# Gate projections by seven block products, and the inner rows' transposes moved into the experts' products

## The reference

```python
proj = u @ w_in                                   # u: 640 x 1024
qkv, z, b_raw, a_raw, hy, gates = jnp.split(proj, _split_points(IN_SPLITS), -1)
...
gate_a, gate_b = jnp.split(jax.nn.sigmoid(gates), 2, -1)          # 2 x 1024 channels
mixed = (gate_a * (o_a @ w_up_a) + gate_b * (o_b @ w_up_b)) @ w_out
...
hid = jax.nn.silu(jnp.einsum('becd,edf->becf', xs, w_gate)) * jnp.einsum('becd,edf->becf', xs, w_up)
ys = jnp.einsum('becf,efd->becd', hid, w_down) * aff[..., None].astype(u.dtype)
```

## Time and profile before

| | |
|---|---|
| Times of the kernel before | 1490.21 us median of 3 runs (1488.09 to 1490.8) |
| Profiled execution | 1486.47 us, span 1484.7 us |
| TensorE busy | 1385.1 us (93% of the span) |
| VectorE busy | 562.7 us (38%) |
| ScalarE busy | 247.1 us (17%) |
| HBM traffic | 201 GB/s over the span |
| Mean granted TensorE clock | 0.978 |

### The profile page before, as it was taken

How to read it: one execution, slowest core, us unless ns; L and a number is a source line. 1 busy time by engine, 2 the same in 40 slices (tenths; PEclk the granted TensorE clock), 3 DMA queues, 4 the chain that set the end, 5 groups by cost and what they waited for, 6 DMA issues and landing times.

```text
span 1484.7 us, 24301 instructions
## 1 busy us (share of the span) xinstructions
PE 1385.1 (93%) x10696; PEld 746.9 (50%) x10696; DVE 562.7 (38%) x1258; ACT 247.1 (17%) x479; POOL 71.3 (5%) x63
## 2 busy tenths in 40 slices
PE   6999999998999999999999984999999999999991
PEld 2455554657888875556555442443433433433430
DVE  5223237546666641103003675222233322222236
ACT  4311122234223332100000022000010000000010
POOL 0000000000000000000000001111111111111110
PEclk9999999999999999999999996999999999999996
DMA  9732212410000001232022046899999999999984
GB/s 383 336 114 105 90 60 86 170 49 24 2 2 2 2 16 48 123 126 115 26 87 76 39 176 266 296 398 388 393 397 400 400 398 395 398 397 392 401 323 152
DMA packets 32027, 298.92 MB, mean 201 GB/s; under 512 B 3435, under 2 KB 7659, under 8 KB 15580
## 3 DMA queue, kind: packets, MB, share of 16 engines
q1 hardware_dynamic: 20876, 270.93, 45.3%
q0 software_dynamic: 7680, 17.11, 4.6%
q10 hardware_dynamic: 3408, 9.96, 1.7%
HBM read 280.69 MB, written 17.30 MB: 201 GB/s over the span
## 4 chain that ended last, share of the span: by engine, by line
PE 64%; DVE 4%; ACT 1%; DMA 1%; issue 1%; DVEq 0%; POOLq 0%
PE bank L531 63%; ACT front L1205 1%; PE bank L926 1%; DVE hbuf L1731 1%; DVE front L1585 0%; DVE hbuf L1881 0%; DVE stats L1879 0%; DMA y_dram<-front,misc 0%; DMA front<-u_dram,misc 0%; DVE misc L1782 0%; PE bank L472 0%; DMA hbuf<-y_dram 0%; DVE misc L1780 0%; DVE front L1783 0%; DVE front L1576 0%
## 5 line engine op out<-in xcount | busy, mean ns | idle before, releaser
L531 PE MATMUL bank<-front,ring 128*128 128x512 f32 (+1 forms) x1736 | 490.6, 443 | 1.8 <-DVE front L1295 0.9
L531 PE MATMUL bank<-ring,front 128*32 128x256 f32 (+3 forms) x3312 | 427.4, 458 | 2.2 <-DVE front L1837 2.2
L531 PEld LDWEIGHTS bank<-front,ring 128*128 128x128 f32 (+1 forms) x1736 | 265.7, 190 | 230.2 <-issue 224.3
L531 PEld LDWEIGHTS bank<-ring,front 128*32 128x32 f32 (+3 forms) x3312 | 178.9, 124 | 248.6 <-issue 208.5
L531 PE MATMUL bank<-front 128*32 128x256 f32 (+3 forms) x2976 | 271.9, 352 | 9.1 <-ACT front L1205 4.7
L531 PEld LDWEIGHTS bank<-front 128*32 128x32 f32 (+3 forms) x2976 | 163.2, 138 | 112.3 <-issue 86.7
L1861 DVE TENSOR_TENSOR front<-bank,front 128x512 f32<-128x512 f32 x16 | 11.1, 691 | 275.3 <-PE bank L531 275.3
L1846 DVE STREAM_TRANSPOSE front<-front 32x256 f32<-32x256 f32 x192 | 83.4, 434 | 5.5
L1374 DVE SCALAR_TENSOR_TENSOR front<-bank,pk,front 128x511 f32<-128x511 f32 x64 | 32.2, 545 | 99.4 <-ACT front L1009 98.8
L1585 DVE COPY_PREDICATED front<-ck,bank 128x256 f32<-128x256 uint32 (+1 forms) x120 | 52.7, 443 | 24.1 <-PE bank L531 21.7
L1201 ACT ACTIVATE front<-bank 128x512 f32<-128x512 f32 x16 | 9.6, 597 | 274.8 <-PE bank L531 274.8
(11 more groups left out here) (274 smaller groups left out, 886.7 us busy)
## 6 DMA issues: line engine op xcount, KB each, us to landing
ring<-w_e_gate_dram SPq DMA_DIRECT2D x32, 2048.0 KB, 15.2
ring<-w_e_up_dram SPq DMA_DIRECT2D x32, 2048.0 KB, 14.7
front<-w_e_down_dram SPq DMA_DIRECT2D x32, 2048.0 KB, 15.4
ring<-w_in_dram SPq DMA_DIRECT2D x11, 2048.0 KB, 7.9
ring<-w_mod_dram SPq DMA_DIRECT2D x10, 2048.0 KB, 12.9
front<-w_mod_dram SPq DMA_DIRECT2D x2, 2048.0 KB, 29.2
ring<-w_out_dram SPq DMA_DIRECT2D x2, 2048.0 KB, 7.6
h_spill<-hbuf ACTq DMA_DIRECT2D x1, 2560.0 KB, 13.8
```

Of the source, the lines that this page charges most:

```text
L531: return pe.matmul(out, lhsT, rhs, start=(k == 0), stop=(k == n - 1))
```

## The change

For the gates, the product of `uT` and a weight half-chunk (256 channels, a "unit") is split into two by two blocks: tokens in two halves of 320, input channels in two halves of 512, output channels in two blocks of 128. Instead of eight block products there are seven (`factors`), each 4 k-steps of 320 columns, taken from sums of blocks: S1 to S4 of the activations, made once, and T1 to T4 of the weights, made for every unit by `weight_sums`. VectorE also adds the seven results into the four blocks of `sig` (`gate_sums`), reading banks 0 to 3 in turn, and ScalarE takes the sigmoids in place. S1 and S2 lie where `h` is loaded back to, so that load is issued after the last product. In the experts, the `hd` transposes go ahead of the sixth k-step of the up `prompt` product, the `hdc` transposes ahead of the third k-step of the down `sample` product; two semaphores become one.

```diff
@@ -278,6 +279,44 @@
         mixedT = reg(W0 + 5120, 5120).rearrange("p (b t) -> p b t", b=KB)
...
+        HT, HK = TOK // 2, KB // 2
+        Z_DONE, GATE_UNITS = 28, 8
+        A11, A12, A21, A22 = (uT[:, HK * j:HK * j + HK, HT * i:HT * i + HT] for i in range(2) for j in range(2))
+        S1, S2 = (hbuf[:, 2560 + HK * HT * i:2560 + HK * HT * (i + 1)].rearrange("p (k t) -> p k t", k=HK) for i in range(2))
+        S3 = A21
+        S4 = misc[:, TOK:TOK + HK * HT].rearrange("p (k t) -> p k t", k=HK)
+        t_areas = [reg(W0 + 7680 + 512 * i, 512) for i in range(5)] + [prompt_f_all[:, 0:512]]
+        t_areas = [a.rearrange("p (k n) -> p k n", k=HK) for a in t_areas]
+        GATES = ("ga0", "gb0", "ga1", "gb1")
+
+        def quadrants(g):
+            w, u = wslot(CH[GATES[g // 2]][0]), g % 2
+            return [[w[:, HK * i:HK * i + HK, P * (2 * u + j):P * (2 * u + j) + P] for j in range(2)] for i in range(2)]
+
+        def column_sums(g):
+            T1, T2, T4 = t_areas[3 * (g % 2):3 * (g % 2) + 3]
+            return T1, T2, quadrants(g)[0][1], T4
+
+        def factors(g):
+            (B11, _, ), (B21, B22) = quadrants(g)
+            T1, T2, T3, T4 = column_sums(g)
+            return (A11, B11), (S2, T2), (S1, T1), (S3, T3), (S4, B22), (A22, T4), (A12, B21)
+
+        def sums_ready(g):
+            return 6 if g == 0 else 12 * g
+
+        def unit_begin(g):
+            return 12 + 12 * g - (4 if g == GATE_UNITS - 1 else 0)
+
+        READ_AT = (1, 2, 5, 4, 6, 7, 8)
+
+        def product_read(n):
+            return unit_begin(n // 7) + READ_AT[n % 7]
+
+        def gate_blocks(g):
+            b = 4 * (g // 2 % 2) + 2 * (g % 2)
+            return [[sig[:, b + j, HT * i:HT * i + HT] for j in range(2)] for i in range(2)]
...
@@ -344,10 +383,10 @@
...
                    ("z", 3, T["w_in"][W_IN_CHUNKS.index(COL_Z)], "proj_mm", 28), mod(9, 2), mod(10, 0),
-                   ("ga0", 1, T["w_in"][W_IN_CHUNKS.index(COL_G)], "proj_mm", 32), ("gb0", 3, T["w_in"][W_IN_CHUNKS.index(COL_G + 1024)], "proj_mm", 36), mod(11, 0),
+                   ("ga0", 1, T["w_in"][W_IN_CHUNKS.index(COL_G)], "proj_mm", 42), ("gb0", 3, T["w_in"][W_IN_CHUNKS.index(COL_G + 1024)], "proj_mm", 56), mod(11, 0),
                    ("upa", 2, T["w_up_a"][0], "up_mm", 8),
                    ("upb", 0, T["w_up_b"][0], "up_mm", 8),
-                   ("ga1", 1, T["w_in"][W_IN_CHUNKS.index(COL_G + 512)], "proj_mm", 40), ("gb1", 3, T["w_in"][W_IN_CHUNKS.index(COL_G + 1536)], "proj_mm", 44),
+                   ("ga1", 1, T["w_in"][W_IN_CHUNKS.index(COL_G + 512)], "proj_mm", 70), ("gb1", 3, T["w_in"][W_IN_CHUNKS.index(COL_G + 1536)], "proj_mm", 84),
@@ -811,13 +850,34 @@
...
+            def gate_unit(g, before={}):
+
+                if g % 2 == 0:
+                    full(GATES[g // 2])
+                for i, (a, b) in enumerate(factors(g)):
+                    n = 7 * g + i
+                    if i in before:
+                        before[i]()
+                    if n >= 4:
+                        pe.wait_ge(sem("sums"), product_read(n - 4))
+                    if i == 1:
+                        pe.wait_ge(sem("sums"), sums_ready(g))
+                    if n == 3:
+                        pe.wait_ge(sem("sums"), 8)
+                    for k in range(HK):
+                        last = mm(bank[n % 4][:, 0:HT], b[:, k, :], a[:, k, :], k, HK)
+                    last.then_inc(sem("proj_mm"), 1)
+
+            pe.wait_ge(sem("zg"), 8)
             for half in range(2):
                 if half:
                     pe.wait_ge(sem("mixed"), 15)
                     spread_gate(pe, mm, 0)
                     pe.wait_ge(sem("mixed"), 20)
-                project(f"ga{half}", {n: o_hook(n) for n in range(HEADS)} if half == 0 else {})
-                project(f"gb{half}", {1: lambda: mod_product(11, "og", 3 * HEADS), 3: lambda: mod_transpose(11)} if half == 0 else {})
+                hooks = [{}] * 4 if half else [{2: o_hook(0), 5: o_hook(1)}, {1: o_hook(2), 4: o_hook(3)},
+                                               {3: lambda: mod_product(11, "og", 3 * HEADS)}, {3: lambda: mod_transpose(11)}]
+                for u in range(4):
+                    gate_unit(4 * half + u, hooks[u])
@@ -828,7 +888,7 @@
                 for b in range(4):
                     n = 4 * half + b
                     if b == 1:
-                        pe.wait_ge(sem("zg"), 2 * (12 + 8 * half))
+                        pe.wait_ge(sem("sums"), unit_begin(4 * half + 3) + 8)
...
@@ -899,39 +959,48 @@
...
-                def sample(out, xT, s):
+                def sample(out, xT, s, before={}):
 
                     for k in range(KB):
+                        if k in before:
+                            before[k]()
                         if k % 4 == 0:
...
-                def prompt(out, xT, s):
+                def prompt(out, xT, s, before={}):
 
                     for k in range(KB):
+                        if k in before:
+                            before[k]()
...
-                sample(bank[0], xsT, 0).then_inc(sem("gate_mm"), 1)
+                sample(bank[0], xsT, 0).then_inc(sem("inner_s_mm"), 1)
                 prompt(bank[2][:, 0:256], xcT, 0).then_inc(sem("gu_mm"), 1)
-                sample(bank[1], xsT, 2).then_inc(sem("up_e_mm"), 1)
+                sample(bank[1], xsT, 2).then_inc(sem("inner_s_mm"), 1)
                 pe.wait_ge(sem("ysc"), e + 1)
-                prompt(bank[5][:, 256:512], xcT, 2).then_inc(sem("gu_mm"), 1)
-                pe.wait_ge(sem("hid_e"), e * 2 + 1)
-                for j in range(4):
-                    i = pe.transpose(bank[6][:, P * j:P * j + P], hd[:, P * j:P * j + P], ident)
-                i.then_inc(sem("hidT_mm"), 1)
-                pe.wait_ge(sem("hid_e"), e * 2 + 2)
-                for j in range(2):
-                    i = pe.transpose(bank[2][:, 256 + P * j:256 + P * j + P], hdc[:, P * j:P * j + P], ident)
-                i.then_inc(sem("hidT_mm"), 1)
+
+                def sample_inner():
+                    pe.wait_ge(sem("hid_e"), e * 2 + 1)
+                    for j in range(4):
+                        i = pe.transpose(bank[6][:, P * j:P * j + P], hd[:, P * j:P * j + P], ident)
+                    i.then_inc(sem("hidT_mm"), 1)
+
+                def prompt_inner():
+                    pe.wait_ge(sem("hid_e"), e * 2 + 2)
+                    for j in range(2):
+                        i = pe.transpose(bank[2][:, 256 + P * j:256 + P * j + P], hdc[:, P * j:P * j + P], ident)
+                    i.then_inc(sem("hidT_mm"), 1)
+
+                prompt(bank[5][:, 256:512], xcT, 2, {5: sample_inner}).then_inc(sem("gu_mm"), 1)
                 pe.wait_ge(sem("hidT"), e + 1)
                 pe.wait_ge(sem("ys"), e + 1)
-                sample(bank[7], hdT, 4).then_inc(sem("down_s_mm"), 1)
+                sample(bank[7], hdT, 4, {2: prompt_inner}).then_inc(sem("down_s_mm"), 1)
                 pe.wait_ge(sem("hidTc"), e + 1)
                 prompt(bank[5][:, 0:256], hdcT, 4).then_inc(sem("down_mm"), 1)
@@ -1160,15 +1229,15 @@
...
-            for half in range(2):
-                for b in range(8):
-                    if half == 0 and b == 5:
-                        mod_rows(11)
-                    gate(CONV + 4 + 8 * half + b, ACT.Sigmoid, sig[:, b, :])
-                if half == 0:
-
-                    act.wait_ge(sem("og"), 3 * HEADS)
-                    act.dma_start(h, h_spill.rearrange("p (t d) -> p t d", t=NT)).then_inc(sem("h_back"), 16)
+            for g in range(GATE_UNITS):
+                c = gate_blocks(g)
+                if g == 3:
+                    mod_rows(11)
+                for n, (i, j) in enumerate(((1, 1), (0, 1), (1, 0), (0, 0))):
+                    act.wait_ge(sem("sums"), unit_begin(g) + 5 + n)
+                    A(c[i][j], c[i][j], ACT.Sigmoid).then_inc(sem("zg"), 1)
+            act.wait_ge(sem("proj_mm"), Z_DONE + 7 * GATE_UNITS)
+            act.dma_start(h, h_spill.rearrange("p (t d) -> p t d", t=NT)).then_inc(sem("h_back"), 16)
@@ -1197,7 +1266,7 @@
...
-                act.wait_ge(sem("gate_mm"), e + 1)
+                act.wait_ge(sem("inner_s_mm"), e * 2 + 1)
                 A(sil, bank[0][:, :], ACT.Silu).then_inc(sem("sil"), 1)
@@ -1656,19 +1725,94 @@
...
+            def weight_sums(g):
+                s, value = CH[GATES[g // 2]]
+                dve.wait_ge(slot_full[s], value)
+                if g >= 2:
+                    dve.wait_ge(sem("proj_mm"), Z_DONE + 7 * (g - 1))
+                (B11, B12), (B21, B22) = quadrants(g)
+                T1, T2, T3, T4 = column_sums(g)
+                subtract(T1, B12, B11)
+                sums.settle()
+                subtract(T2, B22, T1)
+                subtract(T3, B22, B12)
+                sums.settle()
+                subtract(T4, B21, T2)
+                assert sums.n == sums_ready(g)
+
+            def gate_sums(g, between={}):
```

(86 more changed lines are left out.)

## The result

The changed kernel takes **1476.45 us** (median of six, 1474.45 to 1480.95), the kernel before 1489.2 in runs beside it (six, 1487.85 to 1491.34): a ratio of **0.9928** with a 95% interval of 0.9913 to 0.9942. The time is the forecast one, 1476.4, within 0.1 us. The step is not: 13.8 us were forecast, the two medians differ by 12.75, and the ratio, which gives less than the medians do, is worth 0.0072 x 1490.21 = 10.7 us. What is off is one term above all, the experts, forecast 2.9 us too large; a clock term of 1.7 us that did not occur in the profiled execution hides part of it.

What follows compares the result with a forecast made beforehand. TensorE was taken to bound the kernel, with the DMA a second limit just behind in the experts. Gates -17.2, waits +5.2, clock +1.7 and experts -3.5 gave -13.8 us: from 1490.21 to 1476.4, range 1470 to 1483.5.

Steps and rivals of the forecast that it cites:

- a clock term of 1.7 us: Second lifts: after 3.2 us idle, TensorE's clock falls to half and loses 1.7 us; bounds 0 and 1.7.
- Products and waits: Gates: shorter products remove 17.2 us; three new TensorE waits of 0.9, 1.1 and 3.2 give back 5.2.
- the 4.1 us into unit 3: Gates: when the `ga1` load lands, 12.2 us after issue, leaving 1.6 us of margin, so no cost.
- the second rival: Gates: `ga1` comes late, its load taking 18.0 us and overrunning the margin by 4.2; 1480.6 us, chance 0.15.
- So TensorE saves 0.31 to 0.69 us an expert: Experts: the 1.35 us gap goes, six inserted transposes cost 0.66 to 1.04; 5.0 to 11.0 us over sixteen.
- about 6.0 us ahead: Experts: the most TensorE can be ahead when the last down product begins, limited by weight landings.
- The 33.5 us itself: Experts: time the DMA needs per expert, 33.24 + 0.28 from growing landing times, more than TensorE.
- the prediction's own sign of being wrong: Experts: the forecast is wrong if weight landings come closer together than 33.5 us.
- The tail: Last expert: VectorE's xT work starts later, so the last `ys` comes 2.5 us later relative to the down product.
- The third rival: Experts: inserted transposes save nothing and the tail loses 2.5 us; 7.8 saved in all, 1482.4 us, chance 0.15.
- The first: Experts: the DMA keeps up, saving 8.5 us there and 18.8 in all; 1471.4 us, chance 0.15.
- The fourth: Experts: xT becomes the bound ahead of each gate product; 1507.8 us if L, its lateness, is 3.0; chance 0.05.

Runs made afterwards that it cites:

- the run with 8.27 us: Changed kernel with eight more copies of the gate row ahead of the four that the second lifts wait for; 1483.01 us, a single run.
- the run with the waits off the path: Changed kernel with first spread ahead of the `zg` wait, mod column inside the unit's sums, gate-row copies ahead of the second half's sums; 1469.72 us, ratio 0.9861.
- the run in which TensorE waits for weights: Changed kernel with the last two of eight k-steps of the `prompt` products left out, loads all there; last experts' `ys` 33.13 to 33.20 us apart.
- `ys` first: On top of the run with the waits off the path: xT's modulation behind `ys` on VectorE, `prompt` rows' transposes one step earlier; 1467.46 us, ratio 0.9853.

## Why the prediction was right, and where it was not

**Products and waits: right, each by its own number.** 2.163 us a product was forecast, 2.153 measured; 56 of them are 120.6 us against 138.4, -17.8 (forecast -17.2). The waits were forecast at 0.9, 1.1 and 3.2, together 5.2; they are 1.09, 0.97 and 2.98, together 5.04, each released by the instruction that the prediction named. Taking them off the path gave 5.8 us, so they were the path. From z to the output projection the sum -12.0 stands against -12.07. That it fits so well is in part luck: the products gave 0.6 us more than forecast, and the idle times cost 5.5 us by the count above where 5.2 were forecast; -17.8 + 5.5 = -12.3 leaves 0.2 us unexplained. `ga1` landed 12.4 us after its issue (forecast 12.2; the 4.1 us into unit 3 hold 0.5 for the issue, which the text there does not name). It was never waited for by TensorE, and the second rival falls.

**The clock: the size was right, the event is not certain.** One fall of 3.4 us costs 250.95 - 249.29 = 1.7 us, the forecast term; one of 6.8 costs 2.95. In the profiled execution there was none, so this term is 0 there, and the gates did better than the sum with it by 1.8. Over the seven executions it is (1.66 + 2.94 + 2.96) / 7 = 1.1 us on average. The Trainium skill (TensorE: Matmul & The Clock Gate, "Why this matters for your kernels") warns of falls after idle gaps; the run with 8.27 us agrees, the idle time of 2.98 us only in three executions of seven.

**The experts: the failed step is "So TensorE saves 0.31 to 0.69 us an expert".** The gap of 1.35 us went, as forecast. But the six transposes that now stand inside the products cost 33.07 - 31.89 = 1.18 us, above the upper bound of 1.04, and 0.17 us was left. The bounds were the durations of dense transposes, and of the transposes on the chain; neither holds the two changes of the array's form for both groups (the 0.60 holds one, 0.16 above the dense 0.44). By the experiments two groups cost 2 x 0.29 and six transposes 6 x 0.11, 1.24 us, near the measured 1.18. What followed on this step had no footing: "about 6.0 us ahead", cut off by the DMA. TensorE came to be 2.7 us ahead (16 x 0.17; 3.2 from the output projection to the last down product, 636.61 to 633.39), too little for the DMA to bind: it waits for no weights. The 33.5 us itself was read from landing times that grow from expert to expert; they grow in the changed kernel, but not in the run with the waits off the path at the same 33.07 us an expert. There the prediction's own sign of being wrong occurs, landings closer together than 33.5 us.

**The tail: right.** +2.5 us was forecast, 10.02 - 7.41 = 2.61 measured, and the mechanism, VectorE's xT work ahead of `ys`, is shown by the run that puts part of it behind `ys`. Net, the experts' part is worth 0.8 us in the changed kernel's profile, 1.1 in its own (from the first expert's first product), and nothing that the times can tell from zero by itself, against 3.5. The third rival, that the inserted transposes save nothing and the experts lose 2.5 us, is about as far off as the forecast, on the other side: 0.17 us an expert were saved, against 0 there and 0.31 to 0.69 here. The first, a DMA that keeps up, needed 33.24 - 0.69 = 32.55 us an expert; in the run in which TensorE waits for weights it stays at 33.1 to 33.2. The fourth did not occur: xT held nobody up.

**The time and the step.** Gates -12.1 and experts with their tail -0.6 are -12.7, without a fall of the clock. Not all of it stays: the profiled span is 10.1 us shorter, since the work ahead of z ended 1.45 us later in this execution and what follows the last `ys`, the transfers above all, took 1.1 us more. Timed, the change is worth 10.7 us by the ratio (8.6 to 13.0 by the interval) and 12.75 by the medians. That the forecast time is met to 0.1 us while the forecast step is 1 to 3 us too large is luck: two errors, 2.9 us in the experts and 1.7 in the clock, have opposite signs, and the rest is a matter of the medians: 1490.21 in the runs shown ahead, 1489.2 beside the changed kernel, and six runs of it that spread over 6.5 us.

## What to carry to other kernels

Where a kernel is bound by TensorE, fewer products pay in full, but look at what each queue does between the last new instruction and the next wait of TensorE: here 5 of 17 us went back to three waits that cost three moved blocks of code to remove. Moving small full-array transposes into column-tiled products costs by the group, here about 0.29 us inside a product and half of it where the tiles change anyway, beside 0.11 for each transpose: it pays only if the gap that it removes is longer than groups and transposes together (here a gap of 1.35 us went and 1.18 us came back). And when an instruction is delayed within a loop whose iterations hide it, look at the last iteration, which has nothing to hide it under.

## What the runs showed that was not expected

- A change between full-array and column-tiled matmuls shows no idle time in the timeline; it shows only as a longer chain: 0.29 us for a group inside a product (33.07 to 33.36 with no instruction added), 0.16 at a place with a change of its own.
- After the same idle time of 2.98 us the granted clock fell in three executions of seven, for 3.4 or 6.8 us, and the stretch with it is 1.7 or 2.95 us longer; where it did not fall, four executions agree within 0.04 us.
- With all DMA engines busy (share 1.02) an expert's loads and adds took 33.2 us where TensorE waited for them. In the profiles before and after, weights landed 33.5 to 33.6 us apart on average at the same share, in that of `ys` first 33.2 to 33.3, with the waits off the path 33.1 to 33.2; why the spacing differs between executions of nearly the same loads stays open.
